# Attention blocks in a two-layer encoder trunk: maxima of a block ahead of the division of the block before, probabilities copied ahead of mixed values

## What is computed

```python
def sink_softmax(s, sink):
    sk = sink.astype(jnp.float32)[..., None]
    m = jnp.maximum(jnp.max(s, axis=-1, keepdims=True), sk)
    p = jnp.exp(s - m)
    return p / (jnp.sum(p, axis=-1, keepdims=True) + jnp.exp(sk - m))

# meta tokens see the 16 meta keys; each chunk of 64 frames sees them, its own chunk and the one before
s_meta = jnp.einsum('bcqkgd,bmkd->bcqkgm', qr, km)
s_win = jnp.einsum('bcqkgd,bcnkd->bcqkgn', qr, kw)
p = sink_softmax(jnp.concatenate([s_meta, s_win], axis=-1), sk)
o_r = (jnp.einsum('bcqkgm,bmkd->bcqkgd', p[..., :N_META], vm)
       + jnp.einsum('bcqkgn,bcnkd->bcqkgd', p[..., N_META:], vw))
...
h = h + jnp.concatenate([attn, pool], axis=-1) @ w_out[l]
```

## Time and profile before

| what | value |
|---|---|
| median of 3 runs (lowest, highest) | 1105.76 us (1100.26, 1106.54) |
| profiled execution: own time | 1100.07 us |
| profiled execution: span, first to last instruction | 1098.3 us |
| mean granted TensorE clock, share of full speed | 0.988 |
| PE busy | 1064.2 us, 97% of the span |
| DVE busy | 522.4 us, 48% |
| ACT busy | 471.3 us, 43% |
| GpSimd (POOL) busy | 123.3 us, 11% |
| chain that ended last, by engine | PE 82%, ACT 8%, DVE 7% |

### The profile page before, as it was taken

How to read it: one execution, slowest core, us unless ns; L and a number is a source line. 1 busy time by engine, 2 the same in 40 slices (tenths; PEclk the granted TensorE clock), 3 DMA queues, 4 the chain that set the end, 5 groups by cost and what they waited for, 6 DMA issues and landing times.

```text
span 1098.3 us, 18457 instructions
## 1 busy us (share of the span) xinstructions
PE 1064.2 (97%) x7668; PEld 1001.0 (91%) x7668; DVE 522.4 (48%) x690; ACT 471.3 (43%) x662; POOL 123.3 (11%) x121
## 2 busy tenths in 40 slices
PE   6998899999999999999999989999999999999997
PEld 6897799999999999999999978999988999888886
DVE  5667645545445545232336576455455544532221
ACT  5775435444444444122237664364344543421110
POOL 1262000111000111000003510000001100000000
PEclk9989999999999999999999899999999999999999
DMA  6311222322322322323321112223223232233212
GB/s 201 103 49 40 77 77 77 103 89 77 114 76 76 105 86 70 103 78 105 104 78 49 39 40 97 96 77 108 84 76 114 77 111 80 76 106 106 72 61 77
DMA packets 93518, 94.30 MB, mean 86 GB/s; under 512 B 3392, under 2 KB 91800, under 8 KB 93480
## 3 DMA queue, kind: packets, MB, share of 16 engines
q1 hardware_dynamic: 92768, 93.01, 26.4%
q0 software_dynamic: 400, 0.58, 0.2%
q10 hardware_dynamic: 312, 0.18, 0.1%
HBM read 91.65 MB, written 2.10 MB: 85 GB/s over the span
## 4 chain that ended last, share of the span: by engine, by line
PE 82%; ACT 8%; DVE 7%; issue 1%; DMA 1%; SPq 0%; POOL 0%; DVEq 0%; ACTq 0%; POOLq 0%
PE slot L443 80%; ACT probs L919 3%; ACT w_hi L337 1%; DVE nmax L1170 1%; DMA x_in<-in_x 1%; ACT rot_s L844 1%; DVE ms_work L1121 1%; DVE probs L1189 1%; DVE w_lo L348 1%; DVE mix_lo L1205 0%; ACT x_hi L778 0%; DVE den L1181 0%; DVE sumsq L1046 0%; DVE sink_arg L1175 0%; ACT pool_hi L852 0%
## 5 line engine op out<-in xcount | busy, mean ns | idle before, releaser
L443 PE MATMUL slot<-x_hi,w_hi 128*128 128x264 f32 (+1 forms) x1552 | 364.1, 302 | 5.4 <-DVE x_lo L1033 2.7
L443 PE MATMUL slot<-x_lo,w_hi 128*128 128x264 f32 (+1 forms) x1552 | 361.0, 300 | 0.0
L443 PE MATMUL slot<-x_hi,w_lo 128*128 128x264 f32 (+1 forms) x1552 | 360.2, 299 | 0.0
L348 DVE TENSOR_TENSOR w_lo<-raw,w_hi 128x2048 fp32r<-128x2048 f32 (+2 forms) x87 | 194.6, 2237 | 247.6 <-ACT w_hi L337 247.6
L337 ACT ACTIVATE w_hi<-raw 128x2048 fp32r<-128x2048 f32 (+3 forms) x89 | 160.8, 1806 | 260.8 <-PE slot L443 259.5
L443 PEld LDWEIGHTS slot<-x_hi,w_hi 128*128 128x128 f32 x1552 | 254.4, 190 | 17.4 <-DVE u_sb L1152 3.9
L443 PEld LDWEIGHTS slot<-x_lo,w_hi 128*128 128x128 f32 x1552 | 253.0, 190 | 7.3
L443 PEld LDWEIGHTS slot<-x_hi,w_lo 128*128 128x128 f32 x1552 | 252.6, 191 | 7.4
L443 PE MATMUL slot<-m_hi,w_lo 128*128 128x264 f32 (+1 forms) x528 | 140.7, 321 | 0.0
L443 PE MATMUL slot<-m_hi,w_hi 128*128 128x264 f32 (+1 forms) x528 | 140.4, 320 | 0.0
L443 PE MATMUL slot<-m_lo,w_hi 128*128 128x264 f32 (+1 forms) x528 | 140.3, 320 | 0.0
(11 more groups left out here) (142 smaller groups left out, 931.3 us busy)
## 6 DMA issues: line engine op xcount, KB each, us to landing
raw<-in_w_gate SPq DMA_DIRECT2D x44, 512.0 KB, 4.6
raw<-in_w_up SPq DMA_DIRECT2D x44, 512.0 KB, 4.4
raw<-in_w_down SPq DMA_DIRECT2D x32, 512.0 KB, 4.3
raw<-in_w_in SPq DMA_DIRECT2D x19, 512.0 KB, 4.9
raw<-in_w_out SPq DMA_DIRECT2D x16, 512.0 KB, 4.5
raw<-in_w_down SPq DMA_DIRECT2D x16, 384.0 KB, 3.6
x_in<-in_x SPq DMA_DIRECT2D x4, 512.0 KB, 7.7
out<-y_out SPq DMA_DIRECT2D x8, 256.0 KB, 3.0
```

The lines of the kernel that those rows point to most:

```text
L348: ins = nc.vector.tensor_tensor(w_lo[s][:, a:b], raw[s][:, a:b], w_hi[s][:, a:b].bitcast(f32), ALU.subtract)
L443: ins = nc.tensor.matmul(out_part, w[ws][:, r, cols], a[:, k, tokens], start=first and n == 0 and w is w_hi and a is a_hi, stop=end and w ...
```

## The change

Two pieces of code are moved, each within its engine's loop over the steps. On DVE, the maxima of block s come first in step s, the division of block s-1 comes ahead of the lo part of block s-3's mixed values, and in step 9 the pooling mixer's three pieces come behind the division. On ACT, the copy of the probabilities comes ahead of the hi part of the mixed values. PE's program, POOL's and SP's are the same, and no instruction is added or taken away.

```diff
@@ ACT
                 for step in range(NB + 3):
+                    if 2 <= step < NB + 2 and step != NB:
+                        probs_out(step - 2)
                     if step >= 3 and step != NB:
                         heads_hi(step - 3)
-                    if 2 <= step < NB + 2 and step != NB:
-                        probs_out(step - 2)
@@ DVE
                 for step in range(NB + 3):
+                    if step < NB:
+                        row_maxima(step)
                     if 3 <= step < NB + 2:
                         meta_probs_out(step - 2)
+                    if 1 <= step <= NB:
+                        divide(step - 1)
                     if step >= 3:
                         heads_lo(step - 3)
                     if step == NB:
                         pool_map_lo(1)
                         pooled_lo(2)
                         pooled_tile(3)
-                    if 1 <= step <= NB:
-                        divide(step - 1)
-                    if step < NB:
-                        row_maxima(step)
```

## The result

| | before | changed |
|---|---|---|
| runs | 4 | 4 |
| median, us | 1103.01 | 1130.22 |
| lowest to highest, us | 1099.05 to 1106.54 | 1126.96 to 1136.15 |
| profiled execution: own time, span, us | 1100.07, 1098.3 | 1126.96, 1125.2 |
| granted clock, mean | 0.988 | 0.977 |

The ratio is 1.0254, with a 95% interval of 1.019 to 1.0317. The forecast was 1125.0, between 1110 and 1142, slower with a chance of 0.86. The profiled execution rose by 26.9 us where the sum had 22.5.

A forecast was written before the change was run, and what follows sets the result against it. A DVE-ACT loop of 4.9 us plus passings was taken to bound the attention steps. Losses 6.0 + 6.7 + 2.7 + 4.1 + 3.0 = 22.5 us on 1100.07 gave 1122.6; median forecast 1125, range 1110 to 1142.

The forecast's parts named there:

- The loop of one step: Attention steps: PE and DVE take turns, 5.81 us without side rows; six steps 38.5 us, losing 6.0 and 6.7.
- The tail: Scores of block 8 to output projection: 16.7 us over DVE's mixer pieces, against 14.01 and 12.64; 2.7 and 4.1 lost.
- The clock: Attention tails: PE's long pause lowers its clock in both layers, priced at 1.5 us a layer, 3.0 in all.
- the upper price: Tails: the most the clock's fall was put at, 3.4 us a layer, with PE's path overtaking DVE's.
- ACT's part: Probabilities' copy ahead of ACT's hi part: costs nothing under DVE's wait for scores; 8 us if that cover were gone.
- The loops cancel: Attention steps: terms 0.8 us a step too long, steps lose nothing, tail alone costs 7 us: 1107; chance 0.10.
- The opened loop wins: Attention: ACT's idle 2.18 us per step goes, slot 3 does not hold PE, 13.5 us return: 1087; chance 0.04.
- The clock falls within the steps: Attention steps at lower clock: 31 us in all, 1153, or 1138 if through half; chance 0.14.
- The signs: Changed profile: heads wait 1 to 2.4 us, block 7's about 4; maxima wait 2 to 3; nothing changes outside attention.

The follow-up runs named there:

- Lo part first: The changed kernel with DVE's lo part put back ahead of the division, maxima still first: 1111.40 us, ratio 1.0099.
- scores early: The changed kernel with PE's scores of block s+1 moved to the end of step s, behind the transposes: 1116.93 us, ratio 1.0137.
- idle matmuls: The changed kernel with 13 and 28 matmuls that nothing reads, ahead of PE's heads of steps 8 and 9: 1121.32 us, ratio 1.0181.

## Why the prediction was right, and where it was off

**The loop of one step: right in mechanism and size.** It was put at 5.81 us; the chain shows 5.81, and the changed kernel's four steps without side rows behind the transposes take 5.81, 6.01, 5.82 and 5.82. That the two agree to the hundredth is luck: the maxima take 1.35 us in the chain (1.25 in the sum), lo part and passing 0.39 (0.56), heads and transposes 1.99 (1.89), and these cancel. Step by step, from step 2 on, the terms were 5.7, 6.65, 5.81, 7.07, 7.49 and 5.81 us; layer 1 took 5.30, 6.35, 5.82, 6.91, 7.28 and 5.82. Step 2 was 0.4 too long, and a side row is 0.36 (a third of 6.91 less 5.82) and not 0.42, which was read from four rows that began behind a wait (648.40 in the earlier trace rows). Measured, the six come to 37.48 us instead of 38.5: a loss of 5.6 us in layer 1, against 6.7. In layer 0 it was 6.5 against 6.0, since the clock fell once, in step 6, which took 8.59 us; without the 1.5 us of that fall it would be 5.0. Lo part first gives the steps back, scores early gives only the side rows back: both as a loop of this make-up asks.

**The tail: the size at full clock right, and what it runs over only there.** The prediction had 16.7 us, over the mixer's pieces on DVE. With the idle matmuls it is 16.82 over just these pieces. But the changed kernel does not run its tail at full clock. There a path over PE's slower work ends last: in layer 1 heads, map, transposes, ACT's copy and hi part, the lo part; in layer 0 heads, map, ACT's hi part of the map, and of DVE's pieces of the mixer only L1159. The prediction had named such a path as a possibility in the paragraph on the clock and not taken it into the tail's step. That is why moving the pieces back won nothing. At full clock the loss is 2.8 and 4.2 us (16.82 less 14.01 and 12.64), against 2.7 and 4.1.

**The clock: the term that was mis-sized.** The prediction took 1.5 us a layer, 3.0 in all, because it held DVE's chain to be nearly as late. Against the 16.82, the tails of the changed kernel are 2.4 and 4.9 us longer: 7.3. The idle matmuls gave about 6 us of it back in the median. The step of the sum that failed is thus the choice of 1.5 us between the prices 0 and 3.4, for which the only reason was that DVE's chain is there in any case; the upper price, 6.8 for both layers, was nearer. The rule of the Trainium skill ("TensorE: Matmul & The Clock Gate", Part 1), that TensorE's clock is halved after it has been idle, had been priced at that upper value, taken strictly. Measured are 2.4 us in layer 0 and 4.9 in layer 1, below and above the 3.4 a layer. What the estimate missed besides is the extent. I priced the work behind the long pause of 4.20 us. In both layers the clock was down before it, one set of heads earlier, behind a wait of 2.20 us. In layer 0 it fell in the heads of block 6 and was back within the tail (length, PE busy; clock, DMA share, GB/s):

```profile
124.00:125.00 1.00, 0.69 (x6) 1.00 0.00 0
125.00:126.00 1.00, 1.00 (x10) 0.54 0.00 0
...
134.00:135.00 1.00, 1.00 (x6) 0.50 0.00 0
135.00:136.00 1.00, 0.94 (x7) 0.84 0.00 0
...
674.00:675.00 1.00, 0.11 (x1) 0.81 0.00 0
```

In layer 1 it fell between 674 and 675 us, before the heads of block 6 (674.89), and was still down in the output projection (columns as in the earlier trace rows):

```profile
674.00:677.00 3.00, 2.11 (x12) 1.65 (x12) 0.83 (x2) 0.00 (x0) 0.00 (x0) 0.60 0.00 0
677.00:682.00 5.00, 1.42 (x7) 0.93 (x5) 1.23 (x5) 3.83 (x12) 0.00 (x0) 0.50 0.00 0
682.00:687.00 5.00, 4.38 (x22) 3.83 (x23) 3.19 (x6) 1.09 (x2) 0.00 (x0) 0.50 0.00 2
687.00:692.70 5.70, 4.28 (x22) 3.33 (x21) 4.01 (x5) 1.51 (x4) 0.00 (x0) 0.50 0.04 6
692.70:696.00 3.30, 3.30 (x20) 3.30 (x20) 1.30 (x2) 2.50 (x2) 0.00 (x0) 0.64 0.92 312
```

**ACT's part: right, at nothing.** The price without cover was put at 8 us; alone in the old order it is 6.7.

**The rivals.** *The loops cancel* is refuted by the 5.81 us, which are not 0.8 too long. Its condition was also set too low: a loss of 12.7 us over twelve steps needs terms too long by 1.06 us a step, and the 5.3 us that it compares with the bare 5.81 hold side rows; with them the new steps were put at 6.4. *The opened loop wins* needed PE not to wait for slot 3; PE waited 14.8 us for it in layer 0. *The clock falls within the steps* happened once in the twelve steps of the profiled execution, for some 1.5 us (31.14 less 29.60 of PE's busy time), not through half of them. With ACT's order undone, and with the idle matmuls in the tail, step 6 took 8.8 us in both layers and the steps were 1.6 to 3.4 us longer than the changed kernel's, so the rival had something in it: that PE is busy for over half of such a step (6.38 of 8.59 us) did not keep the fall away.

**The total.** The sum had 22.5 us: steps 12.7, tails 6.8, clock 3.0. With the measured terms, steps 6.5 and 5.6, tails at full clock 2.8 and 4.2, clock in the tails 7.3: 26.4 us. The part of attention ahead of block 2 gave 1.3 us back (7.93 and 6.41 us against 7.69 and 7.96), which was not foreseen, and outside attention 1.8 us were lost, which makes the span's 26.9. Of those, 0.64 us lie ahead of the first attention, in code that is the same, 0.13 between the two, and 0.99 behind the second. What caused the first stays open. The last is about what the slow beginning of layer 1's output projection in the rows above costs: its 2.4 us at the lower clock, up to about 695.1, do half as much as at full clock, by estimate 1.2 us lost.

**The signs.** PE's heads waited 0.75 to 2.2 us for the lo part in layer 1's steps 3 to 8 and 4.20 us in step 9, against 1 to 2.4 and about 4; DVE's wait for the scores was 2.4 us on average; PE's free time in the six steps was 7.9 us. "Nothing should change outside" was missed by the 1.8 us.

## What to carry to other kernels

Two in-order engines that feed each other each need an order in which what the other waits for comes first: here the operation that frees a slot ahead of a longer one that nobody waits for yet, and the producer one block ahead of the consumer. Ask of each move what stands ahead of the release that another engine waits for, and write down the whole loop with the new wait in it; here two parts of a change that cost 0.2% and 0.5% alone closed it together and cost 2.5%. Where a move opens a pause on PE, price the clock on all the work up to the next long busy stretch.

## What was not expected of the hardware

The granted clock stayed at the lower level from between 674 and 675 us to about 695 us, though PE was busy for 4.38 of 5.00 us at 0.50 within that time; it was back at 1.00 only in the output projection, where PE is busy without a break. In layer 0 the same heads, map and transposes began at 131.44 at the lower level and had it back at about 135.3, before they ended; in layer 1 they ran slowly from their start at 682.62 to their end at 687.60. The Trainium skill ("TensorE: Matmul & The Clock Gate", Part 1) ties the level to how busy PE has been of late. The rows agree, and show that a tail's work can run slowly for most of its length, and that the same work can have the clock back in one layer and not in the other.

In step 6 of layer 0 the clock fell while PE was already busy again. Its wait of 2.21 us ended at 109.71, and of the stretches behind it the first is at full clock, the second not:

```profile
110.00:111.00 1.00, 1.00 (x13) 0.71 (x13) 1.00 (x2) 0.02 (x1) 0.00 (x0) 1.00 0.00 0
112.00:114.00 2.00, 2.00 (x11) 2.00 (x10) 0.00 (x0) 0.75 (x2) 0.00 (x0) 0.50 0.06 12
```

If the pause is the reason for the fall, it was paid for by work that stands 1.3 us and more behind it; in layer 1 a wait of 2.20 us in the same step was followed by no fall. And with matmuls whose results nobody reads in the pauses, the whole of layer 0's tail was at 1.00.
